# A decoder layer with product-key experts: per-token gathers of u and v rows, against all u and v rows streamed through TensorE

## The reference, cut to what matters

```python
PEER_HEADS, PEER_NKEYS, PEER_TOPK = 8, 128, 16        # 16384 experts, 128 picks per token
q = (hf @ w_q).reshape(T, PEER_HEADS, 2, 128)
s = jnp.einsum('thcd,hckd->thck', q, sub_keys)
s1, i1 = lax.top_k(s[:, :, 0], PEER_TOPK)
s2, i2 = lax.top_k(s[:, :, 1], PEER_TOPK)
cand = (s1[..., :, None] + s2[..., None, :]).reshape(T, 8, 256)
cand_idx = (i1[..., :, None] * PEER_NKEYS + i2[..., None, :]).reshape(T, 8, 256)
top_s, pos = lax.top_k(cand, PEER_TOPK)
expert_idx = jnp.take_along_axis(cand_idx, pos, axis=-1)
weights = jax.nn.softmax(top_s, axis=-1)
act = jax.nn.gelu(jnp.einsum('cd,ced->ce', hc, u[ec]))
out = jnp.einsum('ce,ced->cd', act * wc, v[ec])
```

## Time and profile before

| quantity | value |
|---|---|
| median of 3 runs | 1077.52 us (1076.81 to 1078.42) |
| span of the profiled execution | 1074.3 us, 11042 instructions |
| time outside the span, from the median | 3.2 us |
| TensorE busy | 954.7 us, 89% |
| VectorE busy | 732.4 us, 68% |
| ScalarE busy | 297.0 us, 28% |
| GpSimd busy | 337.1 us, 31% |
| read from HBM | 359.58 MB |

### The profile page before, as it was taken

How to read it: one execution, slowest core, us unless ns; L and a number is a source line. 1 busy time by engine, 2 the same in 40 slices (tenths; PEclk the granted TensorE clock), 3 DMA queues, 4 the chain that set the end, 5 groups by cost and what they waited for, 6 DMA issues and landing times.

```text
span 1074.3 us, 11042 instructions
## 1 busy us (share of the span) xinstructions
PE 954.7 (89%) x3303; PEld 567.7 (53%) x3303; DVE 732.4 (68%) x1933; ACT 297.0 (28%) x811; POOL 337.1 (31%) x325
## 2 busy tenths in 40 slices
PE   7999999999999999899999878787778777778786
PEld 5788888887644675565565433333333323333332
DVE  6699798734456149768748667767678667667554
ACT  3211122254456121523312312212322212212222
POOL 0101003021000015445435644455444454444430
PEclk9999999999999999999999987999889999999899
DMA  9967748886100809999999999999999999999994
GB/s 364 403 248 224 266 150 333 333 306 132 59 20 6 339 32 409 423 384 423 421 422 422 420 423 421 423 424 421 423 423 422 422 423 423 422 423 423 422 423 172
DMA packets 63290, 361.91 MB, mean 337 GB/s; under 512 B 7500, under 2 KB 8156, under 8 KB 30078
## 3 DMA queue, kind: packets, MB, share of 16 engines
q0 software_dynamic: 43280, 292.59, 67.0%
q1 hardware_dynamic: 19950, 68.61, 17.2%
HBM read 359.58 MB, written 1.59 MB: 336 GB/s over the span
## 4 chain that ended last, share of the span: by engine, by line
PE 49%; DMA 35%; DVE 8%; ACT 2%; POOL 2%; issue 2%; SPq 2%; ACTq 0%; POOLq 0%; DVEq 0%
DMA arena<-in_peer_uv,idx 21%; PE pb L553 18%; PE pb L794 14%; DMA ring<-in_peer_uv,idx 10%; DMA qk<-in_peer_uv,idx 2%; PE pb L709 2%; PE pb L679 2%; PE pb L722 2%; PE pb L732 2%; DVE arena L1479 2%; DMA arena<-in_w_ada 2%; PE pb L587 1%; PE pb L774 1%; POOL arena L516 1%; PE pb L823 1%
## 5 line engine op out<-in xcount | busy, mean ns | idle before, releaser
L794 PE MATMUL pb<-arena,sig 128*128 128x512 f32 x416 | 193.3, 616 | 22.4 <-ACT sig L1071 22.4
L794 PE MATMUL pb<-ring,sig 128*128 128x512 f32 x288 | 140.3, 633 | 29.4 <-ACT sig L1071 29.4
L553 PE MATMUL pb<-hT,ring 128*128 128x256 f32 x752 | 162.8, 379 | 0.5 <-ACT arena L899 0.5
L516 POOL DMA_INDIRECT arena<-in_peer_uv,idx x104 | 123.1, 1183 | 113.2 <-PE pb L794 93.1
L1479 DVE CUSTOM_DVE_ANT_0 arena<-arena,sig 128x1024 f32<-128x1024 f32 x104 | 124.4, 1223 | 44.6 <-DMA arena<-in_peer_uv,idx 44.1
L553 PEld LDWEIGHTS pb<-hT,ring 128*128 128x128 f32 x752 | 142.7, 190 | 21.1 <-ACT arena L899 1.7
L794 PEld LDWEIGHTS pb<-arena,sig 128*128 128x128 f32 x416 | 80.9, 197 | 128.9 <-issue 128.7
L1068 ACT ACTIVATE gl<-dot 128x4 f32<-128x4 f32 (+1 forms) x73 | 14.9, 205 | 413.4 <-DVE dot L1479 397.1
L516 POOL DMA_INDIRECT ring<-in_peer_uv,idx x72 | 88.2, 1225 | 91.8 <-PE pb L794 82.4
L1479 DVE CUSTOM_DVE_ANT_0 ring<-ring,sig 128x1024 f32<-128x1024 f32 x72 | 87.7, 1224 | 40.9 <-DMA ring<-in_peer_uv,idx 40.4
L794 PEld LDWEIGHTS pb<-ring,sig 128*128 128x128 f32 x288 | 56.9, 203 | 105.8 <-issue 105.7
(11 more groups left out here) (313 smaller groups left out, 1263.0 us busy)
## 6 DMA issues: line engine op xcount, KB each, us to landing
ring<-in_w_stream SPq DMA_DIRECT2D x79, 512.0 KB, 7.2
arena<-in_w_ada POOLq DMA_DIRECT2D x32, 512.0 KB, 11.7
arena<-in_w_ada SPq DMA_DIRECT2D x12, 512.0 KB, 11.7
arena<-in_w_stream SPq DMA_DIRECT2D x8, 512.0 KB, 6.6
arena<-in_w1k SPq DMA_DIRECT2D x6, 512.0 KB, 8.6
spare<-in_w_stream SPq DMA_DIRECT2D x6, 512.0 KB, 8.5
pair<-in_w_stream SPq DMA_DIRECT2D x5, 512.0 KB
sig<-in_w_ada SPq DMA_DIRECT2D x4, 512.0 KB, 14.8
```

Of the source, the lines that this page charges most:

```text
L516: nc.gpsimd.indirect_dma_start(out=rowat[PLACE[n]], out_offset=None, in_=a["peer_uv"], in_offset=bass.IndirectOffsetOnAxis(ap=idx[:, c, e: ...
L553: last = mm(pb[:, bank, 0:SEQ], w[:, k * P:(k + 1) * P], src[:, k, :], start=(k == 0), stop=(k == DT - 1))
L794: last = mm(pb[:, 4 + 2 * t + hf, :], diag[:, c % DEEP, e, :], rowat[PLACE[n]][:, D + hf * 512:D + (hf + 1) * 512], start=(i == 0 and e == ...
```

## The change

The expert layer no longer gathers. All 16384 rows of u and of v are read once, in order, as 128 + 128 tiles of 512 KB, by SyncE's queue into 9 places (`place_at`).

- Queries: each of the 16 columns is done for token tile 0 and again for tile 1 (32 steps of 8 products 128 x 128 and one score product), all 16 tiles of `w_query` being loaded twice. They all come before the experts.
- u: the keys' second index (i2) runs inside a tile on the partitions, in the layout the host makes; tile i holds the 128 experts of one key i. `keys_pair(q)` multiplies tiles 2q and 2q+1 with all 256 tokens, 8 products 128 x 256 each; `keys_out(q)` writes the gelu of both into `G` (128 partitions x 128 keys x 256 tokens, 128 KB per partition, over the former `arena`, `ring`, `hT`, `y`, `sig` and `sc`, now one tensor `field`).
- Weights: for each token VectorE builds two 128 x 128 matrices with a row per pick: a one-hot of one index, and a one-hot of the other times the softmax weight (`one_hots`, 4 tokens to a group, 64 groups). TensorE multiplies them (`chosen_weights`), which gives the weight of every expert for that token. `weights_in` multiplies this into the gelus that are in `G` already, `weights_out` copies the rest of it to keys that come later, and `keys_in` multiplies the later gelus (kept in `work`) with it. From pair 26 on two groups follow each pair.
- v: `value_rows(i, t)` multiplies `G[:, i, tokens of t]` with v tile i, two products 128 x 512 per token tile, accumulated over 128 tiles. The last 8 tiles (`TAIL`) are done for tile 0 first.
- Retrieval: `head(t, h)` finds the picks, `decode(t)` the indices of a whole token tile at once.

The core of the diff, TensorE first:

```diff
+QS = 2 * PH
+S_U, S_V, STREAM = 2 * QS, 2 * QS + NK, 2 * QS + 2 * NK
+PLACES = 9
+PAIRS = NK // 2
+TG = 4
+NG = SEQ // TG
+FIRST_W, PER = 27, 2
+EXP_AT, TURN_AT = 22, 25
+TAIL = 8
+def groups_after(q):
+
+    lo = min(max(0, PER * (q + 1 - FIRST_W)), NG)
+    return range(lo, min(max(0, PER * (q + 2 - FIRST_W)), NG))
...
+            for n in range(STREAM):
+                if n >= PLACES:
+                    sp.wait_ge(stream_used, n - PLACES + 1)
+                src = a["w_query"][n % QS] if n < S_U else a["peer_u"][n - S_U] if n < S_V else a["peer_v"][n - S_V]
+                sp.dma_start(place_at[n % PLACES], src).then_inc(place_in[n % PLACES], 16)
...
-            for n in range(TT * NE):
...
-                nc.gpsimd.indirect_dma_start(
-                    out=rowat[PLACE[n]], out_offset=None, in_=a["peer_uv"],
...
-            def expert_chunk(c):
...
-                    for hf in range(2):
-                        last = mm(pb[:, 4 + 2 * t + hf, :], diag[:, c % DEEP, e, :],
-                                  rowat[PLACE[n]][:, D + hf * 512:D + (hf + 1) * 512],
...
+            def keys_pair(q):
+                if q >= 2:
+                    pe.wait_ge(a_ge, gelus(q - 1))
+                for i in (2 * q, 2 * q + 1):
+                    n = S_U + i
+                    pe.wait_ge(place_in[n % PLACES], 16 * (n // PLACES + 1))
+                    for k in range(DT):
+                        last = mm(pb[:, q % 2, (i % 2) * SEQ:(i % 2 + 1) * SEQ], place_at[n % PLACES][:, k * P:(k + 1) * P],
+                                  h2T[:, k, :], start=(k == 0), stop=(k == DT - 1))
+                    last.then_inc(stream_used, 1)
+
+            def chosen_weights(g):
+                pe.wait_ge(v_oh, 2 * TG * (g + 1))
+                if g >= 4:
+                    pe.wait_ge(v_w, g - 3)
+                for j in range(TG):
+                    last = mm(pb[:, 2 + g % 4, j * NK:(j + 1) * NK], oh[:, g % 2, 0, j, :], oh[:, g % 2, 1, j, :],
+                              start=True, stop=True)
+                last.then_inc(p_w, 1)
+
+            def value_rows(i, t):
...
+                for hf in range(2):
+                    last = mm(pb[:, 4 + 2 * t + hf, :], G[:, i, t * P:(t + 1) * P],
+                              place_at[n % PLACES][:, hf * 512:(hf + 1) * 512], start=(i == 0), stop=(i == NK - 1))
...
+            for q in range(PAIRS):
+                keys_pair(q)
...
+                for g in groups_after(q):
...
+                    chosen_weights(g)
+            pe.wait_ge(v_w, NG)
+            pe.wait_ge(a_w, NG)
+            for i in range(NK):
...
+            def one_hots(g):
+                for j in range(TG):
+                    t = g * TG + j
+                    V_.tensor_scalar(oh[:, g % 2, 0, j, :], iota[:, :], selT[:, 0, t:t + 1], None, ALU.is_equal
+                                     ).then_inc(v_oh, 1)
+                    V_.tensor_scalar(oh[:, g % 2, 1, j, :], iota[:, :], selT[:, 1, t:t + 1], selT[:, 2, t:t + 1],
+                                     ALU.is_equal, ALU.mult).then_inc(v_oh, 1)
+
+            def weights_in(g):
+                k = keys_before(g)
+                dve.wait_ge(a_w, g + 1)
+                dve.wait_ge(a_ge, gelus(k // 2))
+                dst = G[:, 0:k, g * TG:(g + 1) * TG]
+                V_.tensor_tensor(dst, pb[:, 2 + g % 4, :].rearrange("p (j i) -> p i j", j=TG)[:, 0:k, :], dst, ALU.mult
+                                 ).then_inc(v_w, 1)
+
+            def keys_in(q):
...
+                dst = G[:, 2 * q:2 * q + 2, 0:n]
+                V_.tensor_tensor(dst, temp[:, q % 2, :, 0:n], dst, ALU.mult).then_inc(v_um, 1)
```

More of the change, by code:

```diff
@@ L81, with keys_before, tokens_before, gelus @@
 T_REV, T_W1 = 28, T_V
[L83 to L96, removed]
+QS = 2 * PH
[10 more added lines that the diff above has]
+    return range(lo, min(max(0, PER * (q + 2 - FIRST_W)), NG))
+def keys_before(g):
+    return 2 * (FIRST_W + g // PER)
+def tokens_before(q):
+    return TG * groups_after(q).start
+def gelus(q):
+    return sum((tokens_before(i) > 0) + (tokens_before(i) < SEQ) for i in range(q))
+def mixed(q):
+    return sum(tokens_before(i) > 0 for i in range(q))
 C_BADA, C_GPM, C_GOM, C_GPF, C_GOF, C_CB, C_LG, C_LB, C_CW = 0, 48, 56, 64, 72, 80, 88, 96, 104
@@ L335, in build @@
         ring_in = [sem(f"ring_in{i}") for i in range(RING)] + ada_in[0:DT]
[L336 removed]
+        place_in = [sem(f"place_in{i}") for i in range(PLACES)]
+        stream_used = sem("stream_used")
         a_xh, x1_in, a_hT = sem("a_xhatT"), sem("x1_in"), sem("a_hT")
@@ L1559, in finish_tile @@
                     cs = slice(hf * 512, (hf + 1) * 512)
-                    V_.scalar_tensor_tensor(out=x[:, t, cs], in0=scaled[1][:, cs], scalar=rstd[:, 6 + t:7 + t],
+                    V_.scalar_tensor_tensor(out=x[:, t, cs], in0=scaled[2][:, cs], scalar=rstd[:, 6 + t:7 + t],
                                             in1=x[:, t, cs], op0=ALU.mult, op1=ALU.add).then_inc(v_out, 1)
                 dve.wait_ge(v_out, 2 * (t + 1))
-            first_unit()
+            dve.wait_ge(rows_in, 16)
+            dve.wait_ge(g_const, 4)
+            token_norms(0)
+            h2_turned(0)
+            merged(DT // 2)
+            merged(DT // 2 + 1)
             merged(DT - 2)
             merged(DT - 1)
-            expert_dots(0)
-            for part in range(3):
-                retrieve(1, part)
-            expert_dots(1)
+            head(0, 0)
             token_norms(1)
-            for c in range(2, TT * CPT):
-                k, b = divmod(c, SEG)
-                expert_dots(c)
-                if c == 2:
-                    retrieve(2, 0)
-                if b and k + 2 < UNITS:
-                    retrieve(k + 2, b - 1)
-                if c == CPT + 2:
-                    finish_tile(0)
+            head(0, 1)
+            h2_turned(1)
+            for h in range(2, PH):
+                head(0, h)
+            decode(0)
+            for h in range(PH):
+                head(1, h)
+            softmax_parts()
+            decode(1)
+            softmax_shares()
+            dve.wait_ge(a_selT, 2)
+            one_hots(0)
+            one_hots(1)
+            for q in range(PAIRS):
+                for g in groups_after(q):
+                    weights_in(g)
+                    if g + 2 < NG:
+                        one_hots(g + 2)
+                if tokens_before(q + 1) and q + 1 < PAIRS:
+                    keys_in(q + 1)
+            finish_tile(0)
             finish_tile(1)
```

676 lines of the change are left out of this document (252 added, 424 removed).

## The result

The changed kernel takes 1429.38 us (median of 4, 1428.00 to 1430.38) against 1077.97 us (1076.81 to 1079.35) for the kernel before on the same chip: a ratio of 1.326, 95% interval 1.3245 to 1.3283. The forecast was 1431.0.

What follows compares the result with a forecast made beforehand. Behind 423 us the gathers' DMA bound gives way to TensorE's products: 423.3 + 56.4 + 1.0 + 0.5 + 442.7 + 57.3 + 0.8 + 439.7 + 6.1 = 1427.8 us, plus 3.2 outside the span: 1431 us, range 1424 to 1450 (1423 to 1458 with the first rival's lighter half).

Steps and rivals of the forecast that it cites:

- point where the programs part: Start of the first expert product; everything TensorE waits for before it is unaltered, 423.3 us.
- queries, transposes, copy: 28 remaining query steps 56.4 us, 8 transposes 1.0, wait for the last query's copy 0.5, no longer hidden by gathers.
- keys, one-hots, transposes of the lists: TensorE's u products 442.7 us, 256 tokens' one-hot products 57.3, six transposes of the lists 0.8.
- end: After the last value products: `finish_tile(1)` and the store, same chain as in the old kernel, 6.1 us.
- outside the span: Measured time beyond the profiled span: old span 1074.3 against the runs' median 1077.52, so 3.2 us.
- What bounds the kernel before: TensorE and token mixer chains until some 423 us, then DMA: gathers of 268.4 MB at 414 GB/s, 648 us.
- The price of a product: On TensorE one fp32 product leaves two trace rows: 0.432 us for 256 columns, 0.859 for 512, 0.223 for 128.
- Hidden work: VectorE's retrieval has 90 us of cover; its weights work in pairs 26 to 57 takes 5.3 us under TensorE's 8.70.
- lost clock: Rival: 32 mixed pairs and their waits at clock 0.92 cost 24 us more, 1455 us; 0.09 together with the VectorE case.
- VectorE in the pairs: Rival: slow `weights_in` makes VectorE bind the mixed pairs, 35 us more, 1466 us; 0.09 together with the clock case.
- bound in the stream: Rival: DMA binds the u and v stream, 4.3 us a tile at half the projection's rate, 1654 us; chance 0.01.
- The rival with one row a product: TensorE's two rows overlap, so products behind 423.3 us cost about one row: 965 us; chance 0.01.

Runs made afterwards that it cites:

- before_bf16: The kernel before, with gathers, its 512 value products reading only the upper 16 bits of gathered rows and diagonal weights as bf16: 1075.52 us, ratio 0.9984.
- bf16_pool: bf16_both with all eight unweighted one-hots of a pair made by GpSimd instead of VectorE: 890.42 us.
- half_load: The dense kernel loading only the first half of the columns of each u and v tile, all products as they are: 1428.84 us.
- bf16_both: The dense kernel with key and value products reading only the upper 16 bits of their operands as bf16: 888.89 us, ratio 0.8247.
- bf16_all: bf16_both with the one-hots and the picked weights in them also written as bf16: 888.83 us.
- onehots_thrice: The dense kernel with VectorE making each token's two one-hots three times, output unchanged: 1626.98 us.

## Why the prediction held, step by step

The mechanism came out as forecast, and the small terms missed by up to 2.2 us:

| step of the sum | predicted | measured |
|---|---|---|
| point where the programs part | 423.3 | 425.52 |
| queries, transposes, copy | 57.9 | 57.56 |
| keys, one-hots, transposes of the lists | 500.8 | 499.86 |
| values | 439.7 | 439.48 |
| end | 6.1 | 6.2 |
| outside the span | 3.2 | 1.7 |

Each measured value is the difference of two starts of the chain above. The end is 1428.6 - (982.94 + 439.48) = 6.2 us.

*What bounds the kernel before.* Right. That TensorE was not the bound is shown: half of its busy time taken away gave 1.2 us (before_bf16). That DMA was is read from its share of 1.00, with and without the cheaper products.

*The price of a product.* This was the step that carried the rest, two rows of the trace for one fp32 product, read from starts. 0.2158 and 0.4292 us a row came out against 0.2161 and 0.429. The runs add what the trace of before could not: with bf16 operands a product is one row, of 0.226 us for 512 columns, 3.8 times cheaper than 0.859. The Trainium skill (TensorE: Matmul & The Clock Gate, "Back-to-back issue gap") has two figures for 512 columns, about 131 ns sustained and a formula that gives 216 for a single gap. The run has 0.226 in an unbroken stream of 496, so here the formula is the near one. Four times its 216 is 0.864, an estimate, beside the measured 0.859 of the fp32 product, which is two rows of 0.429 and not the one row that the prediction calls it once.

*Hidden work.* Right, and shown for VectorE by its doubling. One term was too dear: `weights_in` with runs of four elements was feared at a factor of 1.6. Its 256 elements take 422 ns, as long as the contiguous product of as many in the earlier trace rows, 0.42 us. By shape:

```profile
L1406 DVE TENSOR_TENSOR field<-pb,field 128x256 f32<-128x256 f32 x2 | 0.8, 422 | 0.8 <-ACT field L1052 0.8
```

and all shapes together:

```profile
L1406 DVE TENSOR_TENSOR field<-pb,field 128x216 f32<-128x216 f32 (+31 forms) x64 | 32.6, 509 | 16.5 <-ACT field L1052 16.2
```

The 64 of them, 340 elements on the mean, average 509 ns. The one-hots came at 0.455 us a token instead of 0.51. VectorE needed 4.9 us a pair and not 5.3; neither mattered under 8.69.

*Two small errors that in part cancel.* The parting point was 2.2 us late in the profiled execution. Its projection began 0.7 us later (62.98 against 62.25), and from 294.7 to 330.7 us, in attention, the granted clock was 0.95 with 1.5 us lost; of the ten other dense kernels, whose program is the same up to there, nine read 1.00 and part between 423.3 and 424.9, and bf16_pool reads 0.95 and parts near 426. So does before_bf16 (0.95), a kernel with gathers. It is a scatter of executions, not the change; why the clock dips in some is open. And the 3.2 us outside the span came from setting the span of one execution against the median of others. Where both belong to one execution the difference is 1.7 us (1430.29 and 1428.6; for a run of the kernel before, 1078.54 and 1076.8).

*The rivals.* No lost clock (0.998 over the run), no VectorE in the pairs, no bound in the stream (half_load). The rival with one row a product, put at 965 us and 0.01, did not come: every fp32 product here has its two rows. bf16_both has one row a product by other means, of 0.226 us and not 0.429, and takes 889.

## What to carry to other kernels

Before gathers are traded for a dense stream, set the bytes saved against the price of the products added, in starts of trace rows: here 127 MB less, some 300 us of DMA, was bought with 500 us of fp32 products (keys and one-hots) on an engine that had been busy 84% of the stage. The same plan with bf16 products takes 17.5 to 19% less time than the gathers, so the operand type, not the plan, decided the sign; whether cut-off operands will do is the caller's question. When a bound falls, count every cover under it first: retrieval, one-hots and stream all surfaced within one edit. And find the spacing of two starts for each engine in the loop: it gave GpSimd a share, six of eight, that saved 17.8 us at the first attempt. Whether another share is better no run shows; VectorE being full again near the end speaks for a larger one there.

## What the runs showed of the hardware that was not expected

- bf16 products read every second half-word of fp32 data in place, 0.226 us for 512 columns at a clock of 1.00, 5% above a quarter of the fp32 product (0.215).
- GpSimd takes 0.594 us for a one-hot of 128 elements where VectorE's starts are 0.20 us apart for the same operation.
- VectorE writes bf16 from fp32 inputs at the pace of fp32; a result that it must wait for itself costs it 0.12 us.
- TensorE's granted clock fell as its pauses grew, 0.94 to 0.66 (before_bf16) and 1.00 to 0.80 (bf16_all), with no effect that can be seen on the time, since it was not the bound in either. In onehots_thrice, where it waits up to 5.7 us a pair, it reads 0.84 from 670 to 1142 us, and the six pairs behind, with no waits left, take 43.23 us instead of 41.44.
